# Where the first eight modulation chunks land, who scales the first norm, and in which order the first two products run

## The chip, the cores and the metric

The kernel runs on one NeuronCore of a Trainium2 chip. The metric is the device time of one execution in microseconds (us). Five engines with instruction streams of their own work side by side and order themselves by semaphores alone: TensorE (PE), VectorE (DVE), ScalarE (ACT), GpSimd (POOL) and SyncE (SP), which only issues DMAs here. Each matrix is held as two fp32r parts, a high part (the value rounded by a copy) and a low part (what is left), and a product is three matmuls: high times high, low times high, high times low.

## The reference, cut to what matters

Two transformer blocks over 256 tokens of width 1024, float32. The change touches only the beginning of the first:

```python
mod = jax.nn.silu(c) @ w_ada[l] + b_ada[l]                    # 6 x 1024 values
shift1, scale1, gate1, shift2, scale2, gate2 = split(mod, 6)
h = rms_norm(x, norm1_w[l]) * (1.0 + scale1) + shift1
proj = h @ w_in[l]
q, k, v, xBC, z, dt_raw, gates = split(proj, offsets)
```

Only `shift1` and `scale1` are needed before `h`: 2048 of the 6144 modulation columns, 8 MB of `w_ada`. After that come attention, a state-space mixer, a gated sum, an MLP, and the second block.

## The kernel before

All weights come as one stream of 156 chunks of 128 x 2048 float32 (1 MB). `STREAM` (L52 to L56) is its order: eight modulation chunks ("ada"), then the weight chunks ("w") with sixteen more ada chunks between them. The chunks go round a ring of three slots, `raw`; SP issues the first three at once (L407) and each later one (L412) when its slot's semaphore `raw_used` says that the chunk before in it has been used up. A weight chunk is copied to `whi` by ACT (`split`, L561) and its low part `wlo` is made by DVE (`split`, L1059), which frees the slot. PE starts a chunk when its low part is there (`arrived`, L1782).

**The modulation.** DVE's `modulation(i)` (L1074) multiplies the four 512-column parts of chunk i by entries of `csil` (silu of c) and adds them into `acc`: one tensor_scalar (L1091) or scalar_tensor_tensor (L1093) for each part. Two chunks make one unit of 512 columns; PE's `modulation(u)` (L1869) then sums `acc` over the partitions with four one-column matmuls, each of which is two records in the trace. The next but one unit waits for that (`modp_done`). After unit 3, `modulation_out` (L1104) and `scales` (L1111) on DVE make `mod` and `mscale`.

**The norm.** ACT squares x (L574), PE sums the squares (L1834, 16 one-column matmuls, 32 records), ACT takes the root (L578), DVE the reciprocal (`inverse_root`, L1120, which stands between modulation(3) and modulation(4)), and PE spreads it over the partitions (`spread_roots`) into PSUM bank `side[4]`. ACT copies it to `rbs`, and GpSimd multiplies the eight blocks of x by it into `h32` (L500). When `mod` is there, ACT makes the high part `hhi` (L597) and DVE `h0` (L1180) and the low part `hlo` (L1186).

**The first products.** "dt" (chunk 0, of which only 512 columns are used, 24 matmuls over 64 weight columns) and then "q" (chunks 1 to 4), "k" (5), "v" (6): 48 matmuls of 128 x 256 a chunk. PE waits for `hlo` block by block in dt, and the query chunk begins when dt is done. The low part of chunk 1 is made by GpSimd (L505), that of chunk 0 and chunk 2 by DVE, chunk 2 after the last `hlo` (L1188). ACT makes the high parts of chunks 0 and 1 before `first_parts(0)` and that of chunk 2 behind it (L624).

Later in the kernel the second norm of the first block runs by `normed(1)` (L1133): DVE scales a block straight out of PSUM (L1142), ACT makes the high part (L600), DVE the low part (L1148), and PE's `first_pair` (L1819) takes both halves of a chunk block by block.

Of the kernel before, what the change touches and what calls it, by code (L numbers as in the profile page):

```python
# [6 lines left out]
T = 256  # L7
P = 128
# [32 lines left out]
ADA_FIRST = 8  # L41
ADA_BESIDE = ([FIRST["q"] + 1] + [FIRST["z"] + i for i in range(8)]
# [14 lines left out]
assert len(STREAM) % RING == 0 and TURN % (2 * RING) == 0  # L57
assert all((SIZE[n] - PEELED) % TURN == 0 for n in ("m1", "gu")) and ADA_BESIDE[-1] + AHEAD < FIRST["m1"] + PEELED
AT = {k: n for n, k in enumerate(STREAM)}
NR = len(STREAM)  # L60
# [25 lines left out]
def transformer_pair(nc, w_dram, x_dram, cols_dram, tabs_dram, tabs2_dram, out_dram):  # L86
# [69 lines left out]
    h32 = place("h32", [P, KD, T], f32, A0 + 46 * KB)  # L156
    sqx = place("sqx", [P, KD, T], f32, A0 + 54 * KB)
    h0 = place("h0", [P, KD, T], f32, A0 + 54 * KB)
# [3 lines left out]
    rbs = place("rbs", [P, T], f32, A0 + 66 * KB)  # L162
# [75 lines left out]
    with ctx:  # L238
# [19 lines left out]
        def sem(name):  # L258
# [3 lines left out]
        raw_in = [sem(f"raw_in{i}") for i in range(RING)]  # L262
        hi_done = sem("hi_done")
# [56 lines left out]
        sroot_done, srcol_done, srb_done, gsr_done = (  # L320
            sem("sroot_done"), sem("srcol_done"), sem("srb_done"), sem("gsr_done"))
# [82 lines left out]
        @block.sync  # L404
        def _(sp):
            for r in range(RING):
                sp.dma_start(raw[:, r, :], w_dram[r]).then_inc(raw_in[r], 16)  # L407

            with sp.Fori(1, NR // RING) as turn:
                for j in range(RING):  # L410
                    sp.wait_ge(raw_used[j], turn)
                    sp.dma_start(raw[:, j, :],  # L412
                                 w_dram[bass.ds(turn * RING + j, 1)].rearrange("o p n -> p (o n)"))\
                      .then_inc(raw_in[j], 16)
            for m in range(KD):
                sp.wait_ge(res_done, m + 1)
                sp.dma_start(out_dram[m], oute[:, m, :]).then_inc(out_sent, 16)
            sp.wait_ge(out_sent, 16 * KD)
# [3 lines left out]
        def _(pool):  # L422
# [75 lines left out]
            pool.wait_ge(rbc_done, 1)  # L498
            for b in range(KD):
                nc.gpsimd.tensor_tensor(out=h32[:, b, :], in0=xres[:, b, :], in1=rbs[:, :], op=ALU.mult)\  # L500
                  .then_inc(hx_done, 1)

            r = AT["w", 1]
            pool.wait_ge(hi_done, 2)
            nc.gpsimd.tensor_tensor(out=wlo[:, 1, :], in0=raw[:, r % RING, :], in1=whi[:, 1, :].bitcast(f32),  # L505
                                    op=ALU.subtract).then_inc(raw_used[r % RING], 1)
# [36 lines left out]
        def _(act):  # L543
# [43 lines left out]
            def roots_kept(n):  # L587

                act.wait_ge(rb_done, n + 1)
                nc.scalar.activation(rb2[:, :], side[4][:, 0:T], ACT.Copy).then_inc(rbc_done, 1)  # L590

            def first_parts(n):
                buf = h32 if n == 0 else hn
                for b in range(KD):
                    act.wait_ge(hx_done, KD * n + b + 1)
                    if n == 0:
                        ins = nc.scalar.activation(hhi[:, b, :], buf[:, b, :], ACT.Identity,  # L597
                                                   bias=mod[:, b:b + 1], scale=mscale[:, b:b + 1])
                    else:
                        ins = nc.scalar.activation(hhi[:, b, :], buf[:, b, :], ACT.Identity,  # L600
                                                   bias=mod[:, 24 * n + b:24 * n + b + 1])
                    ins.then_inc(h_done, 1)
# [3 lines left out]
            act.dma_start(xres[:, :, :], x_dram).then_inc(x_in, 16)  # L606
            act.dma_start(cols[:, KD:NCOL], cols_dram[:, KD:NCOL]).then_inc(cols_in, 16)
            act.dma_start(tabs[:, 0:P], tabs_dram[:, 0:P]).then_inc(ident_in, 16)
            act.wait_ge(dve_step, 1)
            act.wait_ge(c_in, 16)  # L610
# [5 lines left out]
            act.wait_ge(rb_done, 1)  # L616
            nc.scalar.activation(rbs[:, :], side[4][:, 0:T], ACT.Copy).then_inc(rbc_done, 1)
            split(0)
            act.dma_start(tabs[:, P:NTAB], tabs_dram[:, P:NTAB]).then_inc(tabs_in, 16)
            act.wait_ge(cols_in, 16)  # L620
            split(1)
# [421 lines left out]
        def _(dve):  # L1043
# [30 lines left out]
            def modulation(i):  # L1074

                u, half = i // 2, i % 2
                r = AT["ada", i]
                a = acc[:, u % 2, :]
                dve.wait_ge(raw_in[r % RING], 16 * (r // RING + 1))
                if half == 1:  # L1080
# [4 lines left out]
                for k in range(4):  # L1085
                    kb = 4 * half + k
                    w = raw[:, r % RING, k * 512:(k + 1) * 512]
# [7 lines left out]
                    if k < 3:  # L1095
                        step(ins)
                    else:
# [18 lines left out]
            def inverse_root(n):  # L1116
                dve.wait_ge(root_done, n + 1)
                if n > 0:
                    dve.wait_ge(rb_done, n)
# [12 lines left out]

            def normed(n):  # L1133

                buf = hn
                dve.wait_ge(rb_done, n + 1)
                for b in range(KD + 1):
                    if b < KD:
                        w = mscale[:, KD * n + b:KD * n + b + 1]
                        if b == 0:  # L1140
                            dve.wait_ge(mod_done, 2 + 3 * n)
                        nc.vector.scalar_tensor_tensor(out=buf[:, b, :], in0=xres[:, b, :], scalar=w,  # L1142
                                                       in1=side[4][:, 0:T], op0=ALU.mult, op1=ALU.mult)\
                          .then_inc(hx_done, 1)
                    if b > 0:
                        a = b - 1
                        dve.wait_ge(h_done, KD * n + a + 1)
                        nc.vector.scalar_tensor_tensor(  # L1148
                            out=hlo[:, a, :], in0=buf[:, a, :], scalar=mod[:, 24 * n + a:24 * n + a + 1],
                            in1=hhi[:, a, :].bitcast(f32), op0=ALU.add, op1=ALU.subtract).then_inc(hlo_done, 1)  # L1150
# [11 lines left out]
            for i in range(4):  # L1162
                modulation(i)
            dve.wait_ge(x_in, 16)
            inverse_root(0)
            modulation(4)
# [7 lines left out]

            dve.wait_ge(mod_done, 2)
            scaled = []
            for b in range(KD + 1):
                if b < KD:
                    dve.wait_ge(hx_done, b + 1)
                    scaled.append(step(nc.vector.tensor_scalar(  # L1180
                        h0[:, b, :], h32[:, b, :], mscale[:, b:b + 1], mod[:, b:b + 1], ALU.mult, ALU.add)))
                if b > 0:
                    a = b - 1
                    after(scaled[a])
                    dve.wait_ge(h_done, a + 1)
                    nc.vector.tensor_tensor(out=hlo[:, a, :], in0=h0[:, a, :], in1=hhi[:, a, :].bitcast(f32),  # L1186
                                            op=ALU.subtract).then_inc(hlo_done, 1)
# [230 lines left out]
            dve.wait_ge(srb_done, 1)  # L1418
# [210 lines left out]
            dve.wait_ge(rbc_done, 2)  # L1629
# [105 lines left out]
            dve.wait_ge(rbc_done, 3)  # L1735
# [37 lines left out]
        def _(pe):  # L1773
# [35 lines left out]
            def keep_clock(c, moving, n):  # L1809


                for k in range(n):
                    mm(side[0][:, 0:T], whi[:, c % RING, (k % CB) * P:(k % CB + 1) * P], moving)
# [44 lines left out]
            def modulation_part(u, first, n):  # L1858

                if first == 0:  # L1860
                    r = AT["ada", 2 * u + 1]
                    pe.wait_ge(raw_used[r % RING], use(r))
                for j in range(first, first + n):
# [707 lines left out]
```

## Time and profile before

| | us |
|---|---|
| median of 3 runs | 965.04 |
| lowest, highest | 961.83, 966.72 |
| the profiled execution, device time | 963.45 |
| its span in the trace | 961.7 |
| TensorE busy in the span | 909.5 (95%) |
| VectorE, ScalarE, GpSimd busy | 671.4, 506.6, 105.0 |

The rows of a timeline read: start in us, length in us, engine, line, operation, output <- input, shapes, the number of instructions merged into the row, and in brackets how long the engine had been idle before it and what ended that. Matmul ends are modelled, so the distance from one start to the next says how fast TensorE runs. "L1775" is the line of the helper that issues nearly every matmul, so matmuls are told apart by their tiles.

### The profile page before, as it was taken

The page shows a single profiled execution, that of the slowest core. Times are in us where ns is not written, and L with a number is a line of the kernel's source. Part 1 is how long each engine was busy: PE and PEld are TensorE (multiplying, and loading weights), DVE is VectorE, ACT ScalarE, POOL GpSimd, SP SyncE. Part 2 cuts the span into 40 slices and gives each one's busy share as a digit, 9 for nine tenths or more (in the row PEclk, how much of TensorE's full clock was granted, in tenths as well). Part 3 has the DMA queues.
Part 4 walks back from the last instruction along what each step waited for, and adds up shares of the span by engine and source line. Part 5 has one row for each costly group of instructions (what it writes and reads, how often), then busy time and mean ns, then how long its engine had stood idle before and what let it go on. Part 6 is the DMA issues. An engine that isn't in the chain of part 4 may idle for free.

```text
span 961.7 us, 18261 instructions
## 1 busy us (share of the span) xinstructions
PE 909.5 (95%) x7500; PEld 874.5 (91%) x7500; DVE 671.4 (70%) x916; ACT 506.6 (53%) x686; POOL 105.0 (11%) x75
## 2 busy tenths in 40 slices
PE   4299999999989999999999999999998999999998
PEld 4299999888868789999999999999997999999998
DVE  5864799988658998867976655454785675666642
ACT  2355755566578677334655533435467554444331
POOL 0500045400044533000000000000000000000000
PEclk9999999999999999999999999999999999999999
DMA  9756254476622124676665565645331345555660
GB/s 355 260 215 208 100 176 153 170 252 215 219 88 73 60 88 138 219 286 218 218 231 203 179 213 185 212 137 193 132 132 44 125 139 183 197 189 174 219 197 23
DMA packets 25085, 168.80 MB, mean 176 GB/s; under 512 B 2868, under 2 KB 4532, under 8 KB 4920
## 3 DMA queue, kind: packets, MB, share of 16 engines
q1 hardware_dynamic: 23616, 164.64, 49.5%
q10 hardware_dynamic: 1400, 3.16, 0.9%
q8 instruction: 53, 0.87, 0.4%
q14 instruction: 16, 0.13, 0.0%
HBM read 166.73 MB, written 1.06 MB: 174 GB/s over the span
## 4 chain that ended last, share of the span: by engine, by line
PE 85%; DVE 6%; ACT 5%; issue 2%; DMA 2%; SPq 0%; DVEq 0%; ACTq 0%
PE bank L1775 83%; DVE acc L1093 2%; DMA raw<-w_stream 2%; DVE wlo L1059 1%; ACT whi L561 1%; DVE cvt L1245 1%; PE bank L1990 1%; ACT kw__113 L785 0%; DVE hlo L1186 0%; DVE kw__113 L1352 0%; ACT zt L810 0%; PE bank L2014 0%; ACT sp L876 0%; ACT sp L882 0%; ACT sp L874 0%
## 5 line engine op out<-in xcount | busy, mean ns | idle before, releaser
L1775 PE MATMUL bank<-hhi,whi 128*128 128x256 f32 (+1 forms) x1352 | 387.9, 287 | 9.2 <-DVE hlo L1186 7.0
L1775 PE MATMUL bank<-hhi,wlo 128*128 128x256 f32 (+1 forms) x1352 | 379.1, 280 | 0.0
L1775 PE MATMUL bank<-hlo,whi 128*128 128x256 f32 (+1 forms) x1352 | 379.0, 280 | 0.0
L1059 DVE TENSOR_TENSOR wlo<-raw,whi 128x2048 fp32r<-128x2048 f32 (+1 forms) x130 | 298.1, 2293 | 112.7 <-ACT whi L561 110.6
L561 ACT ACTIVATE whi<-raw 128x2048 fp32r<-128x2048 f32 (+1 forms) x132 | 250.6, 1898 | 99.2 <-PE bank L1775 73.2
L1775 PEld LDWEIGHTS bank<-hhi,whi 128*128 128x128 f32 (+1 forms) x1352 | 255.4, 189 | 16.4 <-issue 14.5
L1775 PEld LDWEIGHTS bank<-hlo,whi 128*128 128x128 f32 (+1 forms) x1352 | 257.3, 190 | 0.3
L1775 PEld LDWEIGHTS bank<-hhi,wlo 128*128 128x128 f32 (+1 forms) x1352 | 256.5, 190 | 0.0
L1775 PE MATMUL bank<-fhi,whi 128*128 128x256 f32 x432 | 120.2, 278 | 0.0
L1775 PE MATMUL bank<-fhi,wlo 128*128 128x256 f32 x432 | 120.1, 278 | 0.0
L1775 PE MATMUL bank<-flo,whi 128*128 128x256 f32 x432 | 120.1, 278 | 0.0
L1775 PEld LDWEIGHTS bank<-flo,whi 128*128 128x128 f32 x432 | 81.9, 189 | 0.0
L1775 PEld LDWEIGHTS bank<-fhi,whi 128*128 128x128 f32 x432 | 81.1, 188 | 0.0
L1775 PEld LDWEIGHTS bank<-fhi,wlo 128*128 128x128 f32 x432 | 81.1, 188 | 0.0
L1093 DVE SCALAR_TENSOR_TENSOR acc<-raw,csil,acc 128x512 f32<-128x512 f32 x84 | 65.5, 779 | 3.2 <-DMA raw<-w_stream 0.4
L1746 DVE TENSOR_TENSOR fr<-bank,rb 128x512 f32<-128x512 f32 x22 | 15.2, 691 | 43.2 <-PE bank L1775 39.9
L1245 DVE SCALAR_TENSOR_TENSOR cvt<-bank,cols,cvt 128x254 f32<-128x254 f32 (+1 forms) x96 | 38.6, 475 | 8.5 <-ACT cvt L672 8.5
L1775 PE MATMUL bank<-onec,acc 128*128 128x1 f32 x96 | 15.1, 276 | 25.0 <-DVE acc L1093 25.0
L1775 PEld LDWEIGHTS bank<-onec,acc 128*128 128x128 f32 x96 | 15.1, 237 | 25.3 <-DVE acc L1093 25.3
L1775 PE MATMUL bank<-sshi,whi 128*128 128x256 f32 x128 | 35.9, 280 | 0.0
L1775 PE MATMUL bank<-sslo,whi 128*128 128x256 f32 x128 | 35.6, 278 | 0.0
L1775 PE MATMUL bank<-sshi,wlo 128*128 128x256 f32 x128 | 35.6, 278 | 0.0
(287 smaller groups left out, 1333.4 us busy)
## 6 DMA issues: line engine op xcount, KB each, us to landing
raw<-w_stream SPq DMA_DIRECT2D x156, 1024.0 KB, 4.9
xres<-x_t ACTq DMA_DIRECT2D x1, 1024.0 KB, 9.8
out<-oute SPq DMA_DIRECT2D x8, 128.0 KB, 3.3
tabs<-tabs_in_dram ACTq DMA_DIRECT2D x1, 641.0 KB, 5.9
tabs<-tabs_in_dram ACTq DMA_DIRECT2D x1, 512.0 KB, 3.6
hankel<-bucket_rows ACTq DMA_DIRECT2D x1, 512.0 KB, 5.9
cols<-cols_in_dram ACTq DMA_DIRECT2D x1, 325.0 KB, 12.7
tabs<-tabs_in_dram ACTq DMA_DIRECT2D x1, 64.0 KB, 12.4
```

The lines of the kernel that those rows point to most:

```text
L561: nc.scalar.activation(whi[:, c % RING, 0:n], raw[:, r % RING, 0:n], ACT.Copy)\
L1059: nc.vector.tensor_tensor(out=wlo[:, c % RING, 0:n], in0=raw[:, r % RING, 0:n], in1=whi[:, c % RING, 0:n].bitcast(f32), op=ALU.subtract)\
L1093: ins = nc.vector.scalar_tensor_tensor(out=a, in0=w, scalar=csil[:, kb:kb + 1], in1=a, op0=ALU.mult, op1=ALU.add)
L1245: ins = nc.vector.scalar_tensor_tensor(out=o, in0=u[:, m * T + lo + s:m * T + hi + s], scalar=col("convw", CONV * f + tap), in1=o, op0=ALU ...
L1746: nc.vector.tensor_tensor(out=fr[:, i % 2, :].rearrange("p (a t) -> p a t", a=2), in0=gemm_bank[(USE["gu"] + i) % 2][:, :].rearrange("p (a ...
L1775: return nc.tensor.matmul(out, lhsT, rhs, start=start, stop=stop)
L1990: last = nc.tensor.transpose(side[2][:, kb * T + t * P:kb * T + (t + 1) * P], prob[:, h % 4, t, kb * P:(kb + 1) * P], tab("ident"))
```

## The change

The first eight modulation chunks get four slots of their own, `adas`, 32 KB per partition that later hold `qt` and others. SP issues chunks 0 and 1, then x (whose DMA leaves ACT's queue), then chunks 2 and 3, and each of chunks 4 to 7 when its slot has been used up (`acc_done`). The ring of three begins with weight chunk 0, of which only 512 columns are loaded, and chunks 1 and 2, all without a wait of their own.

Of chunk 7, DVE sums only the first two parts; PE takes the other two as eight one-column matmuls with the chunk itself as weights and `csil` as the moving column, added up in the same PSUM columns. DVE's `inverse_root(0)` stands behind modulation(4). GpSimd's nine instructions at the start go: DVE scales each block out of PSUM (`scaled_block`), ACT adds the shift for the high part, DVE makes the low part (`second_part`), as `normed(1)` does; DVE also makes the low part of chunk 1, behind the first `hlo`. ACT loads the silu table by a dummy activation before c has arrived. PE gets matmuls whose results nobody reads: `warm` (two of 128 x 512 float32) behind the spread and again behind modulation(3), and `keep_clock` (twelve) behind the first dt block. dt and the first query chunk run block by block together.

```diff
-            for r in range(RING):
-                sp.dma_start(raw[:, r, :], w_dram[r]).then_inc(raw_in[r], 16)
+            for i in range(ADA_FIRST):
+                if i >= ADA_SLOTS:
+                    sp.wait_ge(acc_done, i - ADA_SLOTS + 1)
+                sp.dma_start(adas[:, i % ADA_SLOTS, :], w_dram[i]).then_inc(ada_in[i % ADA_SLOTS], 16)
+                if i == 1:
+                    sp.dma_start(xres[:, :, :], x_dram).then_inc(x_in, 16)
+            n = KD * 2 * NH
+            sp.dma_start(raw[:, 0, 0:n], w_dram[ADA_FIRST, :, 0:n]).then_inc(raw_in[0], 16)
+            for r in range(1, RING):
+                sp.dma_start(raw[:, r, :], w_dram[ADA_FIRST + r]).then_inc(raw_in[r], 16)
...
 GpSimd
-            pool.wait_ge(rbc_done, 1)
-            for b in range(KD):
-                nc.gpsimd.tensor_tensor(out=h32[:, b, :], in0=xres[:, b, :], in1=rbs[:, :], op=ALU.mult)\
-                  .then_inc(hx_done, 1)
-            r = AT["w", 1]
-            pool.wait_ge(hi_done, 2)
-            nc.gpsimd.tensor_tensor(out=wlo[:, 1, :], in0=raw[:, r % RING, :], in1=whi[:, 1, :].bitcast(f32),
-                                    op=ALU.subtract).then_inc(raw_used[r % RING], 1)
...
 ScalarE
-            act.dma_start(xres[:, :, :], x_dram).then_inc(x_in, 16)
             act.wait_ge(dve_step, 1)
+            step(nc.scalar.activation(root[:, 0:1], epsc[:, :], ACT.Silu))
             act.wait_ge(c_in, 16)
...
             root_of(0)
-            act.wait_ge(rb_done, 1)
-            nc.scalar.activation(rbs[:, :], side[4][:, 0:T], ACT.Copy).then_inc(rbc_done, 1)
             split(0)
+            split(1)
             act.dma_start(tabs[:, P:NTAB], tabs_dram[:, P:NTAB]).then_inc(tabs_in, 16)
             act.wait_ge(cols_in, 16)
-            split(1)
             act.wait_ge(mod_done, 2)
             first_parts(0)
             split(2)
...
 VectorE
-                for k in range(4):
+                parts = 2 if i == ADA_FIRST - 1 else 4
+                for k in range(parts):
...
-            for i in range(4):
+            for i in range(5):
                 modulation(i)
-            dve.wait_ge(x_in, 16)
             inverse_root(0)
-            modulation(4)
...
+            dve.wait_ge(rb_done, 1)
             dve.wait_ge(mod_done, 2)
+            scaled_block(0, 0)
+            scaled_block(0, 1)
+            second_part(0, 0)
+            split(1)
+            second_part(0, 1)
+            scaled_block(0, 2)
+            for b in range(3, KD):
+                scaled_block(0, b)
+                second_part(0, b - 1)
+            second_part(0, KD - 1)
             split(2)
...
 TensorE
             spread_roots(rcol, rb_done)
+            warm(xres[:, 0, 0:P], xres[:, 0:2, :], 2)
             modulation(2)
+            pe.wait_ge(csil_done, 1)
+            pe.wait_ge(ada_in[ADA_SLOTS - 1], 16 * ADA_FIRST // ADA_SLOTS)
+            for k in range(2, 4):
+                for j in range(4):
+                    u, at = ADA_FIRST // 2 - 1, k * 512 + j * P
+                    mm(side[5][:, 4 * u + j:4 * u + j + 1], adas[:, ADA_SLOTS - 1, at:at + P],
+                       csil[:, 4 + k:5 + k], k == 2 and j == 0, False)
             modulation(3)
+            warm(xres[:, 0, 0:P], xres[:, 0:2, :], 2)
...
             arrived(0)
+            pe.wait_ge(hlo_done, 1)
+            steps_part(0)
+            keep_clock(0, hhi[:, 0, :], 12)
+            arrived(FIRST["q"])
+            queries_part(0)
+            for kb in range(1, KD):
+                pe.wait_ge(hlo_done, kb + 1)
+                steps_part(kb)
+                queries_part(kb)
```

The rest is bookkeeping: the two semaphores for spread roots become one, the ring's counts begin at the first weight chunk, and the last of its 148 chunks is issued behind the loop.

## Rows read from the trace of the kernel before

**Rows 1.** The page's part on the chain that ended last, shares of the span.

```profile
PE 85%; DVE 6%; ACT 5%; issue 2%; DMA 2%; SPq 0%; DVEq 0%; ACTq 0%
```

**Rows 2.** Whom TensorE waited for, whole span: us in total, times, longest.

```profile
PE bank L1775 <- DVE acc L1093: 25.0, 3, 14.1
PE bank L1775 <- DVE hlo L1186: 7.0, 1, 7.0
```

**Rows 3.** Timeline of VectorE, 0 to 52 us.

```profile
10.88 3.11 DVE L1093 SCALAR_TENSOR_TENSOR acc<-raw,csil,acc 128x512 f32<-128x512 f32 x4 [0.37 <-DMA raw<-w_stream]
14.24 0.49 DVE L1091 TENSOR_SCALAR acc<-raw,csil 128x512 f32<-128x512 f32 x1 [0.25 <-DMA raw<-w_stream]
...
23.20 0.17 DVE L1120 RECIPROCAL rcol<-root 128x2 f32<-128x2 f32 x1 [2.90 <-ACT root L578]
...
40.16 0.17 DVE L1104 TENSOR_TENSOR mod<-bank,cols 128x16 f32<-128x16 f32 x1 [1.30 <-PE bank L1775]
...
42.73 4.27 DVE L1186 TENSOR_TENSOR hlo<-h,hhi 128x256 fp32r<-128x256 f32 x1 [1.43 <-ACT hhi L597]
```

**Rows 4.** The chain that ended last, in order of time: start, us, what.

```profile
33.89 1.11 DVE acc L1093
```

**Rows 5.** Timeline of GpSimd, 0 to 75 us.

```profile
26.07 8.37 POOL L500 TENSOR_TENSOR h<-xres,rbs 128x256 f32<-128x256 f32 x8 [25.62 <-ACT rbs L617]
42.22 4.51 POOL L505 TENSOR_TENSOR wlo<-raw,whi 128x2048 fp32r<-128x2048 f32 x1 [7.78 <-ACT whi L561]
```

**Rows 6.** Timeline of ScalarE, 0 to 82 us.

```profile
6.12 1.28 ACT L611 ACT_TABLE_LOAD   x1 [6.12 <-DMA cols<-cols_in_dram]
40.23 1.91 ACT L561 ACTIVATE whi<-raw 128x2048 fp32r<-128x2048 f32 x1 [3.83 <-DMA raw<-w_stream]
57.46 0.60 ACT L635 ACTIVATE qt<-bank 128x512 f32<-128x512 f32 x1 [3.27 <-PE bank L1775]
80.53 0.60 ACT L635 ACTIVATE kvt<-bank 128x512 f32<-128x512 f32 x1 [1.86 <-PE bank L1775]
```

**Rows 7.** Timeline of TensorE, 0 to 58 us.

```profile
15.83 6.97 PE L1775 MATMUL bank<-onec,sqx 128*128 128x1 f32 x32
24.37 1.20 PE L1775 MATMUL bank<-tabs,rcol 128*128 128x128 f32 x4
38.26 1.87 PE L1775 MATMUL bank<-onec,acc 128*128 128x1 f32 x8 [5.61 <-DVE acc L1093]
47.15 0.45 PE L1775 MATMUL bank<-hhi,whi 128*64 128x256 f32 x1 [7.03 <-DVE hlo L1186]
...
50.63 0.30 PE L1775 MATMUL bank<-hlo,whi 128*64 128x256 f32 x1
...
57.61 0.39 PE L1775 MATMUL bank<-hhi,whi 128*128 128x256 f32 x1
```

**Rows 8.** Stretches: length, PE, PEld, DVE, ACT, POOL busy, PE clock, DMA share, GB/s.

```profile
15.00:20.00 5.00, 5.00 (x25) 5.00 (x25) 4.72 (x7) 0.00 (x0) 0.00 (x0) 1.00 0.99 378
112.00:116.00 4.00, 4.00 (x23) 4.00 (x23) 4.00 (x8) 1.71 (x1) 0.00 (x0) 0.57 0.45 115
```

**Rows 9.** Timelines of VectorE and TensorE around the second norm, 450 to 470 us.

```profile
454.95 0.87 DVE L1142 SCALAR_TENSOR_TENSOR hn<-xres,mscale,bank 128x256 f32<-128x256 f32 x2 [0.97 <-PE bank L1775]
456.07 0.48 DVE L1148 SCALAR_TENSOR_TENSOR hlo<-hn,mod,hhi 128x256 fp32r<-128x256 f32 x1 [0.25 <-ACT hhi L600]
...
461.46 0.48 DVE L1148 SCALAR_TENSOR_TENSOR hlo<-hn,mod,hhi 128x256 fp32r<-128x256 f32 x1 [0.18 <-ACT hhi L600]
463.31 2.29 DVE L1059 TENSOR_TENSOR wlo<-raw,whi 128x2048 fp32r<-128x2048 f32 x1 [1.37 <-ACT whi L561]
...
452.43 1.05 PE L1775 MATMUL bank<-onec,sqn 128*128 128x1 f32 x8
```

**Rows 10.** Timeline of TensorE: after a pause at 109 us, and a float32 matmul of 128 x 512.

```profile
111.39 0.35 PE L1775 MATMUL bank<-hhi,whi 128*128 128x256 f32 x1 [2.11 <-DVE cvt L1245]
...
307.41 1.02 PE L1775 MATMUL bank<-xd,btok 128*128 128x512 f32 x2
```

## What the change will do, predicted from these rows

> **What bounds the kernel now.** I read the chain that ended last first: TensorE carries 85% of it [rows 1], so time is won only where TensorE stands still or works for nothing on the way. The list of whom it waited for comes next [rows 2]: 25.0 us for `acc` and 7.0 us for the first `hlo`, all of it before 47.15, when the first product starts [rows 7]. So the beginning is a serial stretch in which VectorE, not TensorE, is the bound, and everything behind it is moved by whatever moves the start of dense product work. I take as the mark the start of the second query chunk, 57.61 [rows 7]: from there on the instructions are the same in both kernels.
>
> The timelines of the start then show what VectorE loses. It waits 2.90 us for the root before the reciprocal [rows 3], because 32 records of one-column sums (6.97 us) stand on TensorE [rows 7]. Beside GpSimd's eight multiplies, 26.07 to 34.4 [rows 5], one accumulation takes 1.11 us [rows 4], where it is 3.11/4 = 0.78 us alone [rows 3]. The high part of query chunk 0 can't be made before 40.23, since its load comes late through the ring [rows 6]. And the first low part takes 4.27 us [rows 3] beside GpSimd's 4.51 us one [rows 5], where the same kind of step is 0.48 us alone [rows 9].
>
> **The change, part by part. The silu table and the order of the loads: nothing.** The table load, 1.28 us behind c's arrival at 6.12 [rows 6], moves ahead of that arrival, so VectorE starts 1.28 us earlier and has done chunks 0 and 1 by some 12.7 instead of 14.0. But chunk 2 landed only at 14.24 [rows 3], and in both orders the same bytes stand before it (chunks 0 and 1, x, the small tables). VectorE goes on at 14.24, as before; the 1.28 us are lost in a wait. x still lands behind chunk 1, where it did no harm.
>
> **VectorE from 14.24 on.** A chunk costs 0.49 + 3 x 0.78 = 2.85 us if it opens a unit, else 3.11. Chunks 2, 3 and 4: 23.05. The root has long been made (on TensorE the squares start when unit 0 is summed, no later than before), so the reciprocal costs its 0.17 us: 23.2. Chunk 5: 26.35; chunk 6: 29.2; two parts of chunk 7, 1.55 us: 30.8. Before, this was 38.2, when TensorE took the last unit [rows 7]. The 7.4 us are the root wait (2.9), two accumulations (1.55), and GpSimd's company (some eight instructions at 0.33 to 0.46, about 2.9).
>
> **TensorE to the modulation.** Reciprocal 23.2, spread 1.20 us [rows 7]: 24.4. `warm`: nothing in this stretch shows it; the nearest row is a float32 matmul of 512 columns at 0.43 us from record to record, two a matmul [rows 10], so two cost 1.7 us at the 2.4 GHz level. At the 1.2 GHz level, where dt's matmuls go at (50.63 - 47.15)/16 = 0.218 us [rows 7] instead of (80.53 - 57.46)/(4 x 48) = 0.120 [rows 6], they cost 3.1 us. I take 3.1, since 128x1 work before it goes at 6.97/32 = 0.218 too: 27.5. Then 8 + 16 + 8 one-column records: unit 2, the eight matmuls straight from chunk 7, unit 3. At the upper level they cost 1.05/8 = 0.13 each [rows 9], at the lower 1.87/8 = 0.23 [rows 7]. Upper: 28.6, 30.7, then unit 3 once VectorE is done at 30.8, so 31.9. Lower: 29.4, 33.1, 35.0. I take the upper, since the pace rose at 50.63 behind dt's dense work [rows 7], and the first `warm` is dense too. `mod` and `mscale` cost 0.17 each with the hand-over, 0.45: scaling starts at 32.3. Before, the same point was 40.6.
>
> **The norm and chunk 1's low part.** The second norm runs the same three steps: from its first `hn` (454.95) through the last `hlo` (461.46) to the end of the next chunk's low part, 465.60, it takes 10.65 us, a block each 0.77 us, with the high part of that chunk made by ACT only behind the last `hhi` [rows 9]. Here chunk 1's low part stands in it as well, 2.29 us [rows 9]: 12.95, so chunk 2's low part is ready at 45.3. What is queued behind chunk 1's on VectorE are `hlo` 1 to 7, and TensorE waits for them; but it could not use them without that low part. It is ready at 32.3 + 1.6 + 2.3 = 36.2.
>
> **TensorE through dt and the query chunk.** The second `warm` (1.7 to 3.1 us) ends at 33.6 to 35.0, the first `hlo` comes at 33.9. dt's first block and `keep_clock` (15 matmuls, 1.8 to 3.3 us) lie in the wait for chunk 1's low part at 36.2, or pass it by up to 2 us. From there 69 matmuls at 0.120 us are 8.3 us: 44.5. Were it 1 us later it would still be covered, because the next chunk isn't ready before 45.3. So the pairing moves dt out of sight, and the bound is now the chain ACT, VectorE behind the last block. `keep_clock` and `warm` cost nothing on this path as long as these waits cover them; without cover they cost up to 3 us each.
>
> **Loads.** Behind chunk 2 come 5 + 0.25 + 1 MB until query chunk 0 has landed, 6.6 million bytes. At 378 GB/s, the row of the stretch 15 to 20 us [rows 8], that is 17.4 us: 31.7, ACT's copy of 1.91 us [rows 6] ends at 33.6, and VectorE wants it at 33.9. Covered, by 0.3 us only. SP's waits on `acc_done` come early enough: chunk 7 is issued when chunk 3 has been used up, near 20.2, and wanted at 29.2; the weight chunks queued behind that wait lose nothing, since the loads ahead of them keep the engines busy till then.
>
> **The sum.** 57.6 - 45.3 = 12.3 us. Behind the mark each chunk takes TensorE 5.77 us [rows 6] and the split engines 1.91 and 2.29, so that the ring, which now starts with no chunk in hand, catches up by 3.5 us a chunk. The profiled execution, 963.45, becomes 951.15. The median of the runs is 1.59 above that execution, so the time on its scale is 965.04 - 12.3 = 952.7. GpSimd's removal costs nothing: its engine idled from 46.7 to the rope anyway.
>
> **The rivals.**
> 1. The clock. After the first `warm` it may not be up, or fall again, as it did after a pause of 2.11 us at 111.39: the next stretch has a mean grant of 0.57 and 23 matmuls in 4 us [rows 8, 10]. Then unit 3 ends at 35.0, the second `warm` at 38.1, the first block and `keep_clock` at 40 to 41.5, and the 69 matmuls at some 49.3: a gain of 8.3, 956.7. For it: the 6.97 us of one-column sums left the pace at 0.218 to their end [rows 7]. Against: dense float32 work is in it now. The Trainium skill ("TensorE: Matmul & The Clock Gate", Part 1, "What's actually happening") speaks for this rival: it calls the reduced rate the default and says the number of slow matmuls at a start changes from run to run of one kernel. By it runs would lie between 952.7 and 956.7.
> 2. The loads are late: at a rate one tenth lower, chunk 7 is still early, but query chunk 0 lands 1.9 us later, chunk 1's low part moves by 1.6 and all behind it: 954.3. For it: the loads are back to back for 30 us now. Against: no row of the start shows less while SP had work queued.
> 3. The gain is given back in q, k and v. The ring begins with nothing in hand, and modulation(8), 3.1 us on VectorE, stands between low parts; if one of them misses by 2 us and the clock falls, some 4 us go: 956.7. Against: 3.5 us of slack a chunk.
> 4. The change doesn't do what it says: VectorE paces the blocks and pairing hides nothing. At 0.77 us a block against 9 x 0.120 = 1.08 it can't; if it did, dt would stand alone again, 24 x 0.120 = 2.9 us: 955.6.
> 5. Slower than before: the clock stays at the lower level through q, k and v, because every pair waits for a low part. 288 matmuls at 0.098 us more are 28 us, so 981; it decides from 126 slow matmuls on, more than two and a half chunks. Against: 0.218 ended after 16 matmuls [rows 7].
>
> **How the numbers follow.** Forecast 952.7, chance 0.50. The clock 0.25, loads 0.08, given back 0.10 (of which 0.03 within 0.5%), no pairing 0.03, slower 0.02, several together ending within 0.5% 0.02. The range reaches from 949.5 (the forecast on the lowest of the runs of before, 961.83) to 958.0 (rival 1 or 3 with another 1.3 us), which leaves out about 2 in 10. 0.5%, 4.8 us, is about what a measurement of this kernel can tell from no change: faster 0.93, same 0.05, slower 0.02.
>
> **What would show it.** `acc` done by 31, no root wait, every accumulation near 0.75 us; `mod` at 31.9 (rival 1: 35); chunk 1's low part at 36 (rival 2: later, with ACT waiting for the load); nine matmuls a block near 1.1 us; the second query chunk at 45.3 behind a wait of 0.7 us for its low part. Wrong would be: one-column records still at 0.23 us behind `warm`, the mark beyond 47, or a distance from the mark to the end other than 904 us of the span.

## The result, and the profile after

The changed kernel takes 953.38 us in the median of 20 runs (942.67 to 960.93), the kernel before 963.91 us in the median of 20 (954.42 to 971.62). The ratio is 0.9865 with a 95% interval of 0.9838 to 0.9892: 13.0 us of 963.91 are gone, with 10.4 to 15.6 in the interval. The ratio leaves out the slow runs, those more than 1.5% above the fastest of their kernel; the medians of all 20 are 10.5 us apart. The forecast was 12.3 us and 952.7. The profiled execution has a span of 954.9 us.

Whom TensorE waited for in the changed kernel, whole span (us in total, times, longest); these lines answer to [rows 2]:

```profile
PE bank L1788 <- DVE acc L1103: 13.0, 2, 12.7
PE bank L1788 <- DVE cbb L1345: 5.9, 2, 3.9
```

Of 25.0 us of waiting for `acc` 13.0 are left, and the 7.0 us for the first `hlo` have left the list. But a shorter wait isn't yet a shorter path, because TensorE now fills some of that time with matmuls that nobody reads. The path is read from VectorE and from the mark. VectorE in the changed kernel (start, length, engine, line, operation, idle time before it), against [rows 3]:

```profile
6.47 0.49 DVE L1101 TENSOR_SCALAR acc<-adas,csil 128x512 f32<-128x512 f32 x1 [5.56 <-ACT csil L615]
14.55 0.49 DVE L1101 TENSOR_SCALAR acc<-adas,csil 128x512 f32<-128x512 f32 x1 [2.02 <-DMA adas<-w_stream]
23.29 0.16 DVE L1132 RECIPROCAL rcol<-root 128x2 f32<-128x2 f32 x1
27.03 3.97 DVE L1103 SCALAR_TENSOR_TENSOR acc<-adas,csil,acc 128x512 f32<-128x512 f32 x5
30.98 0.68 DVE L1061 TENSOR_TENSOR wlo<-raw,whi 128x512 fp32r<-128x512 f32 x1
32.69 0.17 DVE L1116 TENSOR_TENSOR mod<-bank,cols 128x16 f32<-128x16 f32 x1 [1.03 <-PE bank L1788]
34.73 2.28 DVE L1061 TENSOR_TENSOR wlo<-raw,whi 128x2048 fp32r<-128x2048 f32 x1
44.01 2.29 DVE L1061 TENSOR_TENSOR wlo<-raw,whi 128x2048 fp32r<-128x2048 f32 x1 [1.32 <-ACT whi L568]
```

VectorE starts 1.2 us earlier and stands 2.02 us before chunk 2, which lands at 14.55. From there on it has no gap until its sums are done at 30.9, and `mod` comes at 32.69 instead of 40.16. Chunk 1's low part is ready at 37.0, chunk 2's at 46.3.

TensorE in the changed kernel, against [rows 7]:

```profile
24.58 3.56 PE L1788 MATMUL bank<-xres 128*128 128x512 f32 x4
27.98 0.95 PE L1788 MATMUL bank<-onec,acc 128*128 128x1 f32 x8
28.79 1.93 PE L1788 MATMUL bank<-csil,adas 128*128 128x1 f32 x16
31.05 1.60 PE L1788 MATMUL bank<-onec,acc 128*128 128x1 f32 x8 [0.33 <-DVE acc L1103]
32.51 3.76 PE L1788 MATMUL bank<-xres 128*128 128x512 f32 x4
35.29 1.20 PE L1788 MATMUL bank<-hhi,whi 128*64 128x256 f32 x1
36.71 2.35 PE L1788 MATMUL bank<-hhi,whi 128*128 128x256 f32 x13
38.90 0.28 PE L1788 MATMUL bank<-hlo,whi 128*128 128x256 f32 x1
46.70 0.33 PE L1948 MATMUL bank<-tabs,dtf 64*128 64x64 f32 x2
46.96 0.39 PE L1788 MATMUL bank<-hhi,whi 128*128 128x256 f32 x1
```

The last row is the mark, 46.96, where it was 57.61 before: 10.65 us. TensorE went into it without a wait, 0.66 us after chunk 2's low part was ready. The row at 36.71 holds `keep_clock`'s twelve matmuls and the first one of the query block, which therefore begins near 38.8, 1.8 us after its low part was there.

The granted clock fell within unit 3's sums, the row at 31.05 (stretches of the changed kernel; the clock is the third number from the end):

```profile
31.00:32.00 1.00, 0.95 (x6) 0.95 (x6) 0.66 (x2) 1.00 (x1) 0.00 (x0) 0.69 1.04 376
32.00:33.00 1.00, 1.00 (x5) 0.99 (x5) 0.28 (x2) 0.53 (x1) 0.00 (x0) 0.50 0.82 295
```

Ahead of its first fall this column can't be used: in the changed kernel it shows 1.00 at 16 to 20 us too, where one-column records go at 0.218 us. So for the first 30 us the level is read from the distance between records.

**Why the span alone can't be used.** The mark moved by 10.65 us, but the span by 6.8, from 961.7 to 954.9: behind the mark, where the instructions are the same, the changed kernel took 3.9 us more. The stretch 550 to 575 us shows where (busy times with instruction counts, then granted clock, DMA share, GB/s). The kernel before:

```profile
550.00:575.00 25.00, 25.00 (x223) 25.00 (x222) 11.89 (x9) 11.01 (x9) 0.00 (x0) 1.00 0.55 177
```

The changed kernel:

```profile
550.00:575.00 25.00, 25.00 (x214) 25.00 (x214) 12.23 (x10) 10.46 (x9) 0.00 (x0) 1.00 0.54 189
```

The kernel before, in another execution:

```profile
550.00:575.00 25.00, 25.00 (x215) 25.00 (x214) 11.85 (x10) 11.47 (x10) 0.00 (x0) 1.00 0.63 211
```

The same matmuls at the same granted clock go at 223 or at 215 in 25 us, and the kernel before shows both. Their starts are evenly spaced in both, 0.11 and 0.12 us apart, so no lost records make the difference. So each experiment is read by its mark, and the span only beside it.

### The profile page after: what moved, and what is told of

The parts are those of the page before. It is cut to its first block, busy times and chain, and to the rows that moved or that the text cites. A ratio compares the mean times of both kernels' runs of the same rounds, so it can differ in the third digit from the quotient of the medians.

```text
span 954.9 us, 18288 instructions
## 1 busy us (share of the span) xinstructions
PE 922.9 (97%) x7536; PEld 885.3 (93%) x7536; DVE 666.7 (70%) x915; ACT 506.0 (53%) x686; POOL 92.0 (10%) x66
## 3 DMA queue, kind: packets, MB, share of 16 engines
HBM read 165.95 MB, written 1.06 MB: 175 GB/s over the span
## 4 chain that ended last, share of the span: by engine, by line
PE 86%; DVE 5%; ACT 5%; DMA 2%; issue 2%; SPq 0%; DVEq 0%; ACTq 0%
PE bank L1788 85%; DVE acc L1103 2%; DMA adas<-w_stream 1%; ACT whi L568 1%; DVE wlo L1061 1%; PE bank L2039 1%; DVE cvt L1258 1%; DMA raw<-w_stream 1%; ACT kw__111 L787 0%; DVE kw__111 L1365 0%; ACT zt L812 0%; PE bank L2063 0%; ACT sp L878 0%; ACT sp L884 0%; ACT sp L876 0%
## 5 line engine op out<-in xcount | busy, mean ns | idle before, releaser
L1103 DVE SCALAR_TENSOR_TENSOR acc<-raw,csil,acc 128x512 f32<-128x512 f32 x56 | 42.0, 751 | 1.7
L1788 PE MATMUL bank<-sshi,whi 128*128 128x256 f32 x128 | 36.2, 282 | 0.0
L1029 ACT ACTIVATE ff<-fr 128x256 f32<-128x256 f32 x22 | 9.2, 418 | 43.8 <-DVE fr L1759 43.8
L674 ACT ACTIVATE cvt<-bank,cols 128x256 f32<-128x256 f32 x24 | 12.3, 562 | 36.1 <-PE bank L1788 36.1
## 6 DMA issues: line engine op xcount, KB each, us to landing
xres<-x_t SPq DMA_DIRECT2D x1, 1024.0 KB, 10.4
```

The source lines that it names most:

```text
L674: nc.scalar.activation(cvt[:, i % 2, m, :], u[:, m * T:(m + 1) * T], ACT.Identity, bias=col("convb", f), scale=col("convw", CONV * f + 2))\
L1029: nc.scalar.activation(ff[:, i % 2, 0:T], fr[:, i % 2, 0:T], ACT.Silu).then_inc(fr_done, 1)
L1103: ins = nc.vector.scalar_tensor_tensor(out=a, in0=w, scalar=csil[:, kb:kb + 1], in1=a, op0=ALU.mult, op1=ALU.add)
L1788: return nc.tensor.matmul(out, lhsT, rhs, start=start, stop=stop)
```

## The experiments

All executions that were profiled. "Behind" is the span less the mark, "pace" the TensorE matmuls in 550 to 575 us and in 800 to 825 us. Each row is one execution.

| kernel | mark | `mod` | behind | pace at 550 | pace at 800 |
|---|---|---|---|---|---|
| before | 57.61 | 40.16 | 904.1 | 223 | 214 |
| before, once more | 57.44 | 40.07 | 906.9 | 215 | 223 |
| changed | 46.96 | 32.69 | 907.9 | 214 | 214 |
| changed, once more | 46.84 | 33.05 | 911.8 | 215 | 214 |
| no dummy matmuls | 47.74 | 33.63 | 909.5 | 215 | 214 |
| no second warm | 49.61 | 34.80 | 913.3 | 215 | 214 |
| no keep_clock | 46.57 | 32.91 | 911.9 | 215 | 215 |
| GpSimd kept busy | 50.03 | 35.92 | 903.3 | 214 | 224 |
| dt and query apart | 48.75 | 32.30 | 903.8 | 223 | 214 |
| all sums on VectorE | 49.17 | 34.36 | 895.2 | 223 | 223 |
| reciprocal early | 48.37 | 34.71 | 911.6 | 215 | 215 |
| loads alone, in the kernel before | 56.30 | 43.99 | 904.1 | 223 | 215 |
| x behind chunk 3 | 46.17 | 31.93 | 914.7 | 214 | 215 |

**Does the mark repeat?** Both kernels ran unchanged.

> The changed kernel once more, unchanged, to see how far the mark (the start of the second query chunk, 46.96 us in its trace, 57.61 in that of the kernel before) and the distance from the mark to the end (907.9 and 904.1 us) repeat. Theory A: the mark is set by the order of the beginning and repeats within 1 us, while the distance behind it wanders by 6 us and more with the pace of the dense matmuls in the MLP stretch (215 in 25 us in the one trace, 223 in the other), so the time of one execution can't be used to weigh parts. Rival: the change itself costs some 4 us behind the mark; then the distance is again about 908 and the pace again 215.

> The kernel before once more, unchanged. Its mark should lie at 57.6 within 1 us. Behind the mark it had 904.1 us, with 223 matmuls in each 25 us of the MLP stretch; the changed kernel has shown 903.3 to 913.3 us with 215 there in every look. Theory A: the pace is a matter of the single execution; sooner or later the kernel before shows 215 too, and this look may give 904 to 912 us. Rival: the pace belongs to the kernel; then it is 223 and 904 again, and the change costs some 5 us behind the mark.

The mark repeats within 0.2 us in both kernels. Behind it, kernels with one and the same instructions lie between 895.2 and 914.7 us, and the pace at 550 us is 214 or 215 in nine executions, 223 in four, with the kernel before on both sides. That the change costs some 4 or 5 us behind the mark is refuted, though not by these few executions: the 20 runs of each kernel put the gain at 10.4 us at least, nearly the mark's 10.65. The two columns of pace order the executions: with the faster pace (223 or 224) in both stretches 895.2 us lie behind the mark, with it in one of them 903.3 to 906.9, in neither 907.9 to 914.7. What decides the pace is not shown.

The moment at which VectorE begins chunk 2 also differs, from 14.37 to 14.81 us in the changed kernel and its variants (but for the one with x behind chunk 3). So a difference of single marks carries some 0.2 us that belong to the loads, and where it matters the prices below are also counted from a later row of the same execution.

**GpSimd's company.**

```diff
+            pool.wait_ge(rcol_done, 1)
+            for b in range(KD):
+                nc.gpsimd.tensor_tensor(out=h32[:, b, :], in0=xres[:, b, :], in1=xres[:, 0, :], op=ALU.mult)\
+                  .then_inc(out_sent, 1)
```

(with a wait on ScalarE before the place is used again, and SP's last count raised by eight.)

> The changed kernel with eight multiplies of 128 x 256 on GpSimd whose result nobody reads, begun when the reciprocal is there, as in the kernel before. Theory A (GpSimd's company is what slowed the accumulations): from 23.5 to 32 each of VectorE's accumulations takes 1.10 instead of 0.75 us, VectorE is done with them 2.5 us later, at 33.4, and the mark lies 2 to 2.6 us later, near 49.3. Rival B: the accumulations were slow because of the loads into the ring; then nothing moves.

The timeline of GpSimd in this kernel:

```profile
23.79 8.84 POOL L517 TENSOR_TENSOR h<-xres 128x256 f32<-128x256 f32 x8 [23.34 <-DVE rcol L1138]
```

And that of VectorE beside it:

```profile
23.74 4.04 DVE L1109 SCALAR_TENSOR_TENSOR acc<-adas,csil,acc 128x512 f32<-128x512 f32 x4
27.70 0.94 DVE L1107 TENSOR_SCALAR acc<-adas,csil 128x512 f32<-128x512 f32 x1
28.68 5.29 DVE L1109 SCALAR_TENSOR_TENSOR acc<-adas,csil,acc 128x512 f32<-128x512 f32 x5
```

Four accumulations take 4.04 us instead of 3.11, the tensor_scalar 0.94 instead of 0.48, and VectorE is done 2.97 us later (33.95 against 30.98). Of this 0.26 was there before GpSimd began, as the reciprocal stands at 23.55 instead of 23.29; the company itself costs 2.7. The mark follows by 3.1. Nothing was changed in the loads, so the slow accumulations of the kernel before [rows 4] came from GpSimd. The Trainium skill ("GPSIMD Engine Reference", "8. Key points") says that GpSimd shares its SBUF interfaces with VectorE, whose instructions contend for them when they have two SBUF inputs or run in a 2-port mode. The trace agrees for the accumulations, which have two: 1.1 us against 0.76. The tensor_scalar, which multiplies one tile, went from 0.48 to 0.94; whether it runs in such a mode no run shows.

**The loads alone.** The kernel before with the slots, x behind chunk 1 and the ring begun with the weights; everything else as it was:

```diff
+            for i in range(ADA_FIRST):
+                if i >= ADA_SLOTS:
+                    sp.wait_ge(acc_done, i - ADA_SLOTS + 1)
+                sp.dma_start(adas[:, i % ADA_SLOTS, :], w_dram[i]).then_inc(ada_in[i % ADA_SLOTS], 16)
+                if i == 1:
+                    sp.dma_start(xres[:, :, :], x_dram).then_inc(x_in, 16)
...
```

> The kernel before with the slots and the order of the loads alone: chunks 0 to 7 in slots of their own, x behind the second, the ring begun with the weight chunks; all computation in its old order and on its old engines. Theory A: the accumulations end no earlier than 38 (GpSimd's company and the wait for the root are still there), but the high part of chunk 1 is made by 33, GpSimd makes its low part before the first low parts of the norm instead of beside them, so the first low part comes at 42.7 instead of 47.0 and the mark at 54 to 55.5, 2 to 3.5 us earlier. Rival B: the slots bring the most part of the 10.7 us; then the mark lies below 51.

The mark is at 56.30: 1.2 us earlier, less than either theory said. The high part of chunk 1 was made at 30.72, as expected, but then GpSimd began the low part at 34.18, beside the last accumulations. The chain that ended last (start, length, what) has them:

```profile
33.67 1.10 DVE acc L1117
34.87 4.81 DVE acc L1117
39.70 0.76 DVE acc L1117
```

And GpSimd beside them:

```profile
34.18 4.94 POOL L522 TENSOR_TENSOR wlo<-raw,whi 128x2048 fp32r<-128x2048 f32 x1
```

One accumulation takes 4.81 us, about as long as GpSimd's one instruction of 128 x 2048 (34.18 to 39.12). It is the 4.27 us of the first `hlo` [rows 3], moved to another place: `mod` came 3.9 us later than in the kernel before, at 43.99, and the first `hlo` took 0.43 us. So in the kernel before the early loads are worth little. That they pay with GpSimd out of the way is argued from these rows; no run takes GpSimd out and leaves the loads as they were.

**Where the sums of chunk 7 are made.** The eight matmuls that take the chunk as weights go, and VectorE has `parts = 4` for every chunk.

> The changed kernel with all four parts of modulation chunk 7 summed on VectorE, without the eight matmuls that take the chunk itself as weights. Theory A: VectorE ends its accumulations 1.55 us later, at 32.5; mod comes at 33.9 to 34.5 instead of 32.7 to 33.0, and the mark 0.9 to 1.6 us later. Rival B: the eight matmuls (1.93 us) cost TensorE as much as they save VectorE; then mod and the mark stay.

VectorE takes up chunk 0's low part, its next step, here:

```profile
32.38 0.68 DVE L1061 TENSOR_TENSOR wlo<-raw,whi 128x512 fp32r<-128x512 f32 x1
```

That is 1.40 us later (against 30.98) and, as this execution was 0.16 ahead at the reciprocal, 1.56 by the work itself. `mod` comes 1.3 to 1.7 later and the mark 2.3, more than theory A allowed. Unit 3's sums took 1.87 us here, against 1.60 and 1.87 in the two executions of the changed kernel. The surplus lies on TensorE: `keep_clock` and the first query matmul took 2.59 us against 2.35 and 1.86, and from there to the mark it was 8.5 us against 8.2. So some 0.6 to 1.0 of the 2.3 us isn't the sums' own price.

**The reciprocal's place.**

```diff
-            for i in range(5):
+            for i in range(4):
                 modulation(i)
             inverse_root(0)
-            for i in range(5, ADA_FIRST):
+            for i in range(4, ADA_FIRST):
```

> The changed kernel with the reciprocal back between modulation(3) and modulation(4). The root is ready at 21.6, VectorE is done with chunk 3 at 20.5. Theory A: VectorE waits 1.1 us there and mod and the mark come 1.1 us later, 33.8 and 48.0; the reciprocal's place is worth that, not the 2.9 us of the wait in the kernel before, of which 1.4 went because TensorE began with the squares earlier. Rival B: the spread and the first warm move forward by 1.5 us and TensorE's side gains, so that the mark stays at 46.9.

VectorE in this kernel:

```profile
21.49 0.17 DVE L1132 RECIPROCAL rcol<-root 128x2 f32<-128x2 f32 x1 [1.06 <-ACT root L585]
```

It waits 1.06 us for the root, and its sums end 1.04 us later, 1.2 counted from its start on chunk 2: about what theory A said. `mod` came 1.7 to 2.0 later and the mark moved by 1.5. More than VectorE's share is in that, as the one-column records of units 2 and 3 and of the eight matmuls went at the lower level here, which the next experiment shows as well. So the mark doesn't price the reciprocal's place alone.

**The dummy matmuls.** Three kernels: without all three of them, without the second warm alone, without keep_clock alone.

> The changed kernel without the two warm calls and without keep_clock. Theory A (the clock of TensorE needs them): one-column sums behind the spread run at 0.23 us a record instead of 0.12, mod comes 2 us later, near 35, the nine matmuls a block begin at 0.21 us each, and the mark lies at 49 to 51. Rival B (they are in the way, since TensorE and not VectorE sets the mark in the trace of the changed kernel): the first query block starts when the low part of chunk 1 is there, near 37 to 39, and the mark comes at 46 or earlier.

> The changed kernel without the warm call behind modulation(3) alone; the first warm and keep_clock stay. In the trace of the changed kernel that call took from 32.51 to 36.3, and pushed the first dt block behind the first low part by 1.5 us. Theory A: without it dt's first block starts at 34.8, keep_clock ends at 37 to 37.5, and the mark comes at 46.3, when the low part of chunk 2 is ready: 0.7 us earlier. Rival B: the clock falls in the pause before the first low part, keep_clock and the first blocks run at 0.21 us a matmul, and the mark is 1 to 3 us later.

> The changed kernel without keep_clock alone; both warm calls stay. The prediction said keep_clock lies in the wait for chunk 1's low part and that VectorE's chain sets the mark. In the trace of the changed kernel TensorE was busy with it until 38.9 while that low part was ready at 37.0, and chunk 2's low part was ready 0.66 us before the mark at 46.96. Theory A (TensorE sets the mark): the first query block starts at 37, TensorE is through the 69 matmuls by 45.5, and the mark falls on the end of chunk 2's low part, 46.0 to 46.4. Rival B (keep_clock lifts the clock for the blocks behind it): without it the first blocks run at 0.21 us a matmul until 38 or later and the mark stays at 46.8 or moves back.

The timeline of TensorE in the kernel without the second warm:

```profile
24.52 3.62 PE L1788 MATMUL bank<-xres 128*128 128x512 f32 x4
27.93 1.71 PE L1788 MATMUL bank<-onec,acc 128*128 128x1 f32 x8
29.50 3.55 PE L1788 MATMUL bank<-csil,adas 128*128 128x1 f32 x16
32.91 1.85 PE L1788 MATMUL bank<-onec,acc 128*128 128x1 f32 x8
```

The edit comes behind these rows, and yet they differ from the changed kernel's, where the same 8 + 16 records took 0.95 and 1.93 us. So the first warm didn't lift the clock here. In the eight profiled executions that have this call, it did six times; here and with the reciprocal early it did not. What decides it stays open. That puts `mod` near 34.8 and swamps what the edit was to tell: the second warm's worth stays open, and 34.80 and 49.61 are close to what rival 1 of the prediction worked out, 35.0 and 49.3. Without any dummy the first blocks of one-column sums run at the lower level too, but they start at 26.61 instead of 27.98, so `mod` is only 0.6 to 0.9 later and the mark 0.8 to 0.9. Theory A had said 49 to 51, rival B 46 or less; it lies between. So the dummies are worth 0.8 to 0.9 us when the first warm lifts the clock; when it does not, they cost: `mod` at 34.8 is 1.2 us later than without any of them (33.63).

keep_clock alone is clear, since the rows ahead of it are those of the changed kernel. TensorE in the kernel without it:

```profile
35.51 1.20 PE L1788 MATMUL bank<-hhi,whi 128*64 128x256 f32 x1
37.29 0.39 PE L1788 MATMUL bank<-hhi,whi 128*128 128x256 f32 x1 [0.15 <-DVE wlo L1061]
46.57 0.39 PE L1788 MATMUL bank<-hhi,whi 128*128 128x256 f32 x1 [0.82 <-DVE wlo L1061]
```

The query block starts at 37.29, when its low part is there, at 0.12 us a matmul at once, and the mark now falls on chunk 2's low part after a wait of 0.82 us: 46.57, 0.3 to 0.4 earlier. That time is little more than two executions of one kernel differ by; the wait is the clear sign. In this execution the clock didn't need keep_clock, and in the changed kernel TensorE and not VectorE had set the mark, by 0.66 us in the first execution and by 0.2 in the second.

**dt and the query chunk apart.**

```diff
-            arrived(FIRST["q"])
-            queries_part(0)
             for kb in range(1, KD):
                 pe.wait_ge(hlo_done, kb + 1)
                 steps_part(kb)
-                queries_part(kb)
+            arrived(FIRST["q"])
+            for kb in range(KD):
+                queries_part(kb)
```

> The changed kernel with dt's eight blocks first and the query chunk's eight blocks behind them, the warm calls and keep_clock kept. Theory A: dt is paced by VectorE's low parts and ends near 43, the query chunk takes 48 x 0.115 = 5.5 us, so the mark lies at 48.7 to 49.5, 2 to 2.5 us later than 46.9. Rival B (the low part of chunk 2 sets the mark in both orders): 46.9 to 47.3.

The mark is at 48.75, 1.8 to 1.9 us later, though `mod` came 0.4 to 0.8 earlier than in the changed kernel. From `mod` to the mark it is 2.2 to 2.7 us more, and that is the pairing's worth. The dt blocks then waited for their low parts, most of them like this one, and the query chunk started at 42.7 with all its work before it:

```profile
39.31 0.33 PE L1788 MATMUL bank<-hhi,whi 128*64 128x256 f32 x1 [0.22 <-DVE hlo L1154]
```

**A version meant to beat both.** x behind chunk 3, the reciprocal behind modulation(5), and the dummies moved ahead of unit 0, of the squares and behind unit 1.

```diff
-                if i == 1:
+                if i == 3:
                     sp.dma_start(xres[:, :, :], x_dram).then_inc(x_in, 16)
...
+            pe.wait_ge(cols_in, 16)
+            warm(cols[:, 0:P], cols[:, 0:512], 2)
             modulation(0)
+            warm(cols[:, 0:P], cols[:, 0:512], 3)
...
```

> A version meant to beat both: the changed kernel with x behind chunk 3 instead of chunk 1, so that chunk 2 lands near 12 instead of 14.55 and VectorE's wait of 2.0 us for it goes; the reciprocal stands behind modulation(5). The squares of x then begin near 17 instead of 14.4, so TensorE gets dummy matmuls on the loaded constants ahead of unit 0, ahead of the squares and behind unit 1 (two, three, two of 128 x 512), in place of the warm call behind the spread, to have the squares go at 0.12 us a record instead of 0.22. Theory A: VectorE is done with its accumulations at 28.9 instead of 30.9, mod comes near 30.7, and the mark lies at 43.7 to 45, 2 to 3 us before that of the changed kernel; against the kernel before a ratio near 0.984. Rival B: the clock isn't up while the squares run, they end at 24, unit 1 is summed at 26 and modulation(6) waits for it; then mod comes at 32 to 33 and the mark at 46 to 47. Rival C: the later loads become the bound, chunk 7 or query chunk 0 is waited for, and 1 us of the 2 is lost.

Its ratio to the kernel before is 0.9878 (0.9825 to 0.9930) with 6 and 11 runs: not to be told from the changed kernel's 0.9865. The mark is 46.17, 0.7 to 0.8 earlier, and so in the range of rival B (46 to 47) and not of theory A. VectorE lost its wait before chunk 2 but got another, as its timeline in this version shows:

```profile
12.44 0.48 DVE L1101 TENSOR_SCALAR acc<-adas,csil 128x512 f32<-128x512 f32 x1
19.57 0.49 DVE L1101 TENSOR_SCALAR acc<-adas,csil 128x512 f32<-128x512 f32 x1 [1.07 <-DMA adas<-w_stream]
```

Half of the 2.0 us was lost to chunk 4, which stands behind x now: rival C in kind, though it had named other chunks. The sums ended at 30.1, 0.9 earlier. The squares went in 4.65 us instead of 6.97, so the dummies ahead of them did a part of what they were for; unit 1 behind them went at the lower level again (1.85 us), and a warm of 3.76 us at the lower level stood before dt again.

## Why the prediction was right, step by step

- **The bound.** A serial stretch on VectorE before 47 us set the end; the mark moved by 10.65 us, and the whole became 13.0 us shorter, with 10.4 to 15.6 in the interval. Right. Nothing is given back in q, k and v, as ScalarE copies v's result out at 76.91 instead of 87.56, again 10.65 earlier: rival 3 fell. The forecast of 12.3 lies in the interval, but at the mark, where it can be read exactly, it was 1.7 us too hopeful: 0.9 from `mod`, 0.1 from the norm's chain and 0.7 from TensorE behind it. That the median of 953.38 lies 0.7 us from 952.7 is therefore partly luck.
- **A sign of being wrong that came.** The prediction named "a distance from the mark to the end other than 904 us". It was 907.9 and 911.8. But the kernel before itself has 904.1 and 906.9, so 904 was the value of one execution, and the sign could not tell anything.
- **Loads and the silu table: worth nothing.** Right for VectorE's start: 1.2 us earlier, then a wait of 2.02 us for chunk 2. In the kernel before the loads alone still moved the mark by 1.2. Query chunk 0 landed by 30.62 where 31.7 was worked out, and its high part was made at 32.5 when its low part was begun at 34.73, so the margin was 2.2 us and not 0.3, and rival 2 fell.
- **VectorE.** 30.8 forecast, 30.9 measured. Of its terms, GpSimd's company was put at 2.9 and costs 2.7 when brought back; the two accumulations at 1.55, and cost 1.56; the root wait of 2.9 is, put back alone, 1.06, because TensorE starts the squares 1.5 us earlier than it did (14.37 instead of 15.83), where the forecast had only said "no later than before".
- **TensorE to `mod`.** The one-column records did go at 0.12 us behind the warm call. The term that was mis-sized is unit 3: it began 0.2 us later and took 1.60 instead of 1.05 us, since the clock fell in it (0.69 granted in 31 to 32 us); in the second execution it took 1.87. `mod` came at 32.69 and 33.05, not 31.9. `warm` at the lower level was mis-sized too: its four records took 3.4 us where all ran at that level (24.58 to 27.98), not 3.1.
- **The norm's chain.** From scaling to chunk 2's low part 12.95 us were taken from the second norm and chunk 1's split; it took 13.1 (33.18 to 46.30).
- **The step that failed:** that `warm` and `keep_clock` cost nothing because the wait for chunk 1's low part covers them, "or pass it by up to 2 us". By the forecast's own numbers 2 us were not covered: 36.2 + 2 + 8.3 is 46.5, and chunk 2's low part was to end the cover at 45.3. They passed it by 1.8 us, and so the 69 matmuls and dt's two transposes ended 0.66 us behind chunk 2's low part (0.2 in the second execution). TensorE set the mark, not the chain of ACT and VectorE. The rows point to the second warm: it began 0.6 us later than forecast and ran at the lower level, a row of 3.76 us where at most 3.1 were allowed for. The kernel without it can't show this, as its first warm left the clock down. Taking keep_clock away gave back 0.3 to 0.4.
- **The pairing** was priced at 2.9 us as its own rival; undoing it costs 1.8 to 1.9 at the mark and 2.2 to 2.7 counted from `mod`.
- **Rival 1, the clock.** Not the likeliest, and it did happen: in two of the eight profiled executions with the first warm the clock stayed down and `mod` came about 2 us later. Both were of variants; the two of the changed kernel itself had it up. How many of its 20 runs went that way is not shown.

The parts as the experiments price them, one execution each, against the changed kernel's 46.9: GpSimd 3.1, the sums of chunk 7 2.3 (1.56 on VectorE), the pairing 1.9, the reciprocal 1.5 (1.0 to 1.2 on VectorE, the rest with the clock down), the dummies 0.8. They depend on one another, as the loads show, which alone bring 1.2, with one accumulation held for 4.81 us by GpSimd.

## What to carry to other kernels

A helper's instruction can cost another engine time even when nobody waits for the helper, as GpSimd's did VectorE here: look for one operation whose time differs from place to place, and at what runs beside it. Weigh a part of a change by the moment at which the work behind it starts, not by the span, when one and the same kernel's spans differ by more than the part. Dummy matmuls that are to hold the clock stand on the path themselves as soon as they run at the lower level; give them the cover that they need at that level, or leave them out. And set a possible overrun against the cover in numbers: 2 us of it against 0.8 of cover was already a path of its own.

## What the runs showed of the hardware that was not expected

A VectorE instruction beside one long GpSimd instruction isn't slowed by a share; it may be held until that one ends: 4.81 us instead of 0.76 beside 4.94 us on GpSimd, 4.27 instead of 0.41 beside 4.51 [rows 3, 5]; both ended 0.3 to 0.6 us after GpSimd's. Beside eight short GpSimd instructions of about 1.1 us each accumulation took 1.1 us.

One and the same run of fp32r matmuls of 256 columns goes at 214, 215 or 223 in 25 us with a granted clock of 1.00 each time. It holds for long stretches of an execution and may differ between stretches: the kernel before had 223 at 550 us and 214 at 800 us in one execution, 215 and 223 in the next. It goes with the time behind the mark, 895.2 us with the faster pace in both stretches and 907.9 to 914.7 with it in neither. What decides it stays open.

One and the same call of two float32 matmuls of 512 columns, behind the same instructions, left TensorE's clock up in six executions and down in two. In the six it fell again between 30 and 32 us, before the next such call, and that call ran at the lower level in all six.
